# Strassen's scheme for most of the up projection, in a hybrid decoder step on one core: w_up by 7 block products in place of 8, w_up and w_down as two passes

## What is computed

```python
x = x + gt1 * mix                      # mix = merged @ w_out, 1024 x 1024
h = _rmsnorm(x, g2n) * (1 + sc2) + sh2
x = x + gt2 * (jnp.square(jax.nn.relu(h @ w_up)) @ w_down)   # w_up 1024 x 4096, w_down 4096 x 1024
y = _rmsnorm(x, g_final)
```

## Time and profile before

| | |
|---|---|
| time, median of 3 runs | 1808.45 us (1806.99 to 1808.63) |
| span of the profiled execution, first to last instruction | 1804.3 us |
| PE busy, in the span | 1775.4 us (98%) |
| VectorE, ScalarE, GpSimd busy | 759.9, 489.3, 12.3 us |
| moved by DMA | 139.34 MB, mean 77 GB/s |
| granted TensorE clock, mean | 0.995 of 2.4 GHz |

### The profile page before, as it was taken

How to read it: one execution, slowest core, us unless ns; L and a number is a source line. 1 busy time by engine, 2 the same in 40 slices (tenths; PEclk the granted TensorE clock), 3 DMA queues, 4 the chain that set the end, 5 groups by cost and what they waited for, 6 DMA issues and landing times.

```text
span 1804.3 us, 26783 instructions
## 1 busy us (share of the span) xinstructions
PE 1775.4 (98%) x10976; PEld 1713.8 (95%) x10976; DVE 759.9 (42%) x1445; ACT 489.3 (27%) x832; POOL 12.3 (1%) x25
## 2 busy tenths in 40 slices
PE   8999999999999999999999989999999999999997
PEld 3899999999999999999999989999999999999997
DVE  3644324444544545333353564343333333433345
ACT  5443333223333233211232341212121121212122
POOL 0000000000000000000000010000000000000000
PEclk9999999999999999999999989999999999999999
DMA  9444544322331232211132111111111111111112
GB/s 310 141 138 156 176 130 131 83 60 69 88 97 54 63 98 58 58 47 46 49 88 79 47 36 47 48 48 46 46 37 45 46 46 46 46 46 46 47 47 97
DMA packets 192677, 139.34 MB, mean 77 GB/s; under 512 B 15323, under 2 KB 176007, under 8 KB 192630
## 3 DMA queue, kind: packets, MB, share of 16 engines
q1 hardware_dynamic: 185910, 130.01, 24.4%
q10 hardware_dynamic: 6720, 8.67, 1.4%
HBM read 120.86 MB, written 17.80 MB: 77 GB/s over the span
## 4 chain that ended last, share of the span: by engine, by line
PE 95%; DVE 2%; DMA 1%; issue 1%; ACT 1%; SPq 0%; DVEq 0%; ACTq 0%
PE PB L916 85%; PE M L844 3%; PE M L969 1%; PE M L860 1%; PE M L1044 1%; DMA araw<-in_w_ada 1%; PE M L1050 1%; PE M L1036 1%; PE M L1038 1%; DVE XL L1223 1%; PE M L908 0%; PE M L1014 0%; DVE R L1709 0%; ACT A L532 0%; PE M L1061 0%
## 5 line engine op out<-in xcount | busy, mean ns | idle before, releaser
L916 PE MATMUL PB<-XH,whi 128*128 128x352 f32 x2496 | 811.3, 325 | 4.1 <-DVE XL L1223 2.1
L916 PE MATMUL PB<-XH,wlo 128*128 128x352 f32 x2496 | 801.5, 321 | 0.0
L916 PE MATMUL PB<-XL,whi 128*128 128x352 f32 x2496 | 801.3, 321 | 0.0
L916 PEld LDWEIGHTS PB<-XH,whi 128*128 128x128 f32 x2496 | 469.0, 188 | 11.3 <-issue 6.9
L916 PEld LDWEIGHTS PB<-XL,whi 128*128 128x128 f32 x2496 | 470.2, 188 | 0.7
L916 PEld LDWEIGHTS PB<-XH,wlo 128*128 128x128 f32 x2496 | 468.7, 188 | 0.0
L550 ACT ACTIVATE whi<-raw 128x1024 fp32r<-128x1024 f32 x134 | 141.3, 1054 | 407.4 <-PE PB L916 404.3
L916 PE MATMUL PB<-AH,whi 128*128 128x352 f32 x720 | 233.1, 324 | 0.2 <-issue 0.2
L916 PE MATMUL PB<-AL,whi 128*128 128x352 f32 x720 | 232.5, 323 | 0.0
L916 PE MATMUL PB<-AH,wlo 128*128 128x352 f32 x720 | 232.1, 322 | 0.0
L1228 DVE TENSOR_TENSOR wlo<-raw,whi 128x1024 fp32r<-128x1024 f32 x134 | 163.7, 1222 | 118.0 <-ACT whi L550 117.1
(11 more groups left out here) (297 smaller groups left out, 1199.4 us busy)
## 6 DMA issues: line engine op xcount, KB each, us to landing
raw<-in_w_in SPq DMA_DIRECT2D x64, 512.0 KB, 4.8
araw<-in_w_ada SPq DMA_DIRECT2D x48, 512.0 KB, 5.3
raw<-in_w_up SPq DMA_DIRECT2D x32, 512.0 KB, 4.0
raw<-in_w_down SPq DMA_DIRECT2D x32, 512.0 KB, 3.4
zp_d<-zr ACTq DMA_DIRECT2D x16, 512.0 KB, 2.7
Z<-zp_d SPq DMA_DIRECT2D x8, 1024.0 KB, 5.8
xin<-in_x_prompt SPq DMA_DIRECT2D x8, 512.0 KB, 7.0
CU<-in_state_C SPq DMA_DIRECT2D x8, 512.0 KB, 3.8
```

The costliest lines, as they stand in the source:

```text
L916: ins = pe.matmul(PB[:, bank, 0:BLK], w[:, w0:w0 + P], x[:, k, a0:a1], start=(k == 0 and j == 0), stop=(k == n_k - 1 and j == 2))
```

## The change

Up to the merge nothing moves. From phase 4 on:

- **Token blocks.** w_out and the first 6 tiles of w_up are computed on four blocks of 264 columns (CB) in place of three of 352: 96 matmuls of 264 columns a tile.
- **Norm.** ScalarE's root of the mean square is taken on a whole 128x264 block after one matmul with `ones` (`mean_square`), and VectorE inverts that block whole (`rstd`); GpSimd takes no part.
- **Strassen's scheme** (in Winograd's form) for the other 26 tiles, 13 pairs: a pair of output tiles by two halves of the contraction by two halves of the tokens (528 columns, two matmuls of 264) needs 7 products of 4 slices in place of 8. The sums of activations (`combo_sum`) are made once, the sums of weights (`w_sums`) per pair; the products are put together in PSUM, with three copies out (`copy_out`, ScalarE) and three sums (`product_sum`, VectorE) per pair.
- **Two passes.** All activations of w_up are written to DRAM (`act_d`, 32 tiles of 128 x 1056), as is the residual (`x2_d`); then w_down runs over all of them in the same 8 rounds of 24 groups, and reloads and splits 4 activation tiles and 4 weight tiles in each.
- The loops of these phases are written out.

```diff
+NCL = 6
+PAIRS = list(range(NCL // 2, FT * 4))
+CLG = [(c, t) for c in range(4) for t in range(4)] + [(c, t) for t in range(4, NCL) for c in range(4)]
...
+    def banks(q, which):
+        b = 4 * ((q + 1) % 2) + 2 * which
+        return PS[:, b:b + 2, 0:CB]
...
@@ SP
+        for q in range(NQ):
+            if 1 <= q < NQ - 1:
+                sp.wait_ge(s["u_lo"], 7 * q)
+                load_pair(q + 1)
+            if q >= 1:
+                sp.wait_ge(s["rl_done"], 4 * q)
+                sp.dma_start(act_d[2 * PAIRS[q - 1]:2 * PAIRS[q - 1] + 2].rearrange("a p n -> p a n"), CST[:]) \
+                  .then_inc(s["pr_out"], 16)
+        last = 7 * (NQ - 1)
+        sp.wait_ge(s["u_lo"], 7 * (NQ - 1))
+        for t in range(2):
+            load_down(t)
...
+        sp.wait_ge(s["wg_done"], last + 3)
+        for j in range(4):
+            load_act(j)
+        sp.wait_ge(s["wg_done"], last + 4)
+        sp.wait_ge(s["x2_out"], 16 * KT)
+        for n in range(4):
+            load_x2(n)
...
+        sp.wait_ge(s["pr_out"], 16 * NQ)
+        for f in range(8):
             for d in range(4):
+                t = 4 * f + d + 2
+                if t < 32:
+                    load_down(t)
+                j = 4 * f + d + 4
+                if 8 <= j < 32:
+                    load_act(j)
@@ GpSimd
-        for i, (b, k) in enumerate(POOL_H2):
...
@@ ScalarE
+        for q in range(NQ):
+            more = q < NQ - 1
+            copy_out(q, 0, T1C, 0, 3)
+            up_hi(q + 1, 0) if more else down_hi(0)
+            copy_out(q, 1, T7C, 1, 2)
+            up_hi(q + 1, 1) if more else down_hi(1)
+            copy_out(q, 2, T2C, 0, 1)
+            if more:
+                for o in range(2, 6):
+                    up_hi(q + 1, o)
+            act.wait_ge(s["wg_done"], 7 * q + 7)
+            if q:
+                act.wait_ge(s["pr_out"], 16 * q)
+            act.activation(halves(CST[:, 0, HB_:T]), banks(q, 0), ACT.Relu).then_inc(s["c12_done"], 1)
+            if more:
+                up_hi(q + 1, 6)
+        for j in range(4):
+            act_hi(j)
@@ TensorE
+        def wide_group(bank, t, c, before=None):
...
+                for j, (w, x) in enumerate(((wh, xh), (wh, xl), (wl, xh))):
+                    ins = pe.matmul(PS[:, bank, 0:CB], w[:, P * k:P * k + P], x, start=(k == 0 and j == 0), stop=(k == KT - 1 and j == 2))
+        def mean_square(c):
+            pe.wait_ge(s["sqa_done"], KT - 1 + c + 1)
...
+            pe.matmul(PS[:, SUMB[c], 0:CB], ones[:], SQA[:, CB * c:CB * c + CB], start=True, stop=True).then_inc(s["sum_done"], 1)
...
+        SEQ = ((0, True), (1, True), (0, False), (1, False), (0, False), (1, True), (0, False))
+        for q in range(NQ):
+            for o, (which, start) in enumerate(SEQ):
+                pe.wait_ge(s["u_lo"], 7 * q + o + 1)
...
+                elif 2 <= o <= 4:
+                    pe.wait_ge(s["cp_done"], 3 * q + o - 1)
+                elif o >= 5:
+                    pe.wait_ge(s["cd_done"], 3 * q + o - 4)
+                bank = banks(q, which)
+                x, wh, wl = combos(o), ring(o, 0), ring(o, 1)
                 for y in range(2):
+                    for k in range(4):
+                        for j, (w, h) in enumerate(((wh, 0), (wh, 1), (wl, 0))):
+                            ins = pe.matmul(bank[:, y, :], w[:, k, :], x[:, h, k, CB * y:CB * y + CB],
...
+        for f in range(7):
+            for n in range(KT):
+                if n % 2 == 0:
+                    pe.wait_ge(s["d_lo"], 4 * f + n // 2 + 1)
+                for b in range(3):
+                    down_group(24 * f + 3 * n + b, f, n, b,
+                               (lambda k: pe.wait_ge(s["al_lo"], 4 * f + k + 1)) if n == b == 0 else None)
@@ VectorE
+        def rstd(c):
+            x = slice(CB * c, CB * c + CB)
+            dve.wait_ge(s["rms_std"], c + 1)
+            link(dve.reciprocal(RSTD[:, x], RSTD[:, x]))
...
+        down_lo(0)
+        act_lo(0)
+        act_lo(1)
+        product_sum(q, 3, T1C, 1, 5, (0, 0))
+        act_lo(2)
+        act_lo(3)
...
+        for f in range(7):
             for d in range(4):
+                for n in (2 * d, 2 * d + 1):
+                    for b in range(3):
+                        accumulate(24 * f + 3 * n + b, n, b)
+                down_lo(4 * f + d + 2)
+                act_lo(4 * f + d + 4)
```

More of the change, by code:

```diff
@@ L82, in layer_kernel @@
     ctx = ExitStack()
-    early, startup, gates, mixer, mlstm, outp, mlp, final = (ExitStack() for _ in range(8))
+    xhs, front, early, startup, gates, mixer, mlstm, late, outp, wino, down = (ExitStack() for _ in range(11))
     def sb(name, shape, dt=F32, scope=ctx):
@@ L220, in layer_kernel @@
[L220 to L224, removed]
@@ L826, in _ @@
-        phase5(0)
-        with act.Fori(1, 7) as f:
-            phase5(f)
-        phase5(7, last=True)
+        wide_hi(T5_ + 2)
+        for k in range(KT):
+            h2_first(k)
+        square(2)
+        std(1)
+        square(3)
+        wide_hi(T5_ + 3)
+        h2_shift(1, 0)
+        h2_copy(1, 0, 1)
+        relu(0)
+        h2_shift(1, 1)
+        h2_copy(1, 1, 2)
+        std(2)
+        relu(1)
+        h2_shift(2, 0)
+        h2_copy(2, 0, 3)
+        relu(2)
+        std(3)
@@ new lines, in copy_out @@
+        def copy_out(q, o, dst, which, read):
+            act.wait_ge(s["wg_done"], 7 * q + o + 1)
+            if q == 0:
+                act.wait_ge(s["u_lo"], 7)
+            else:
+                act.wait_ge(s["cd_done"], 3 * (q - 1) + read)
+            act.activation(halves(dst), banks(q, which), ACT.Copy).then_inc(s["cp_done"], 1)
+        for o in range(7):
+            up_hi(0, o)
+            relu(17 + o)
+        act.wait_ge(s["p4_done"], 32 + len(CLG))
+        combo_hi(2, XB[:, B12, 0], B12)
@@ new lines, in down_group @@
+        def down_group(g, f, n, b, before=None):
+            a0, a1 = BLOCKS[b]
+            t = 4 * f + n // 2
+            if g >= 3:
+                pe.wait_ge(s["dn_free"], g - 2)
+            for k in range(4):
+                if before is not None:
+                    before(k)
+                w0 = 2 * P * k + P * (n % 2)
+                xh, xl = (act_tile(4 * f + k)[:, h, a0:a1] for h in range(2))
+                for j, (w, x) in enumerate(((dhi, xh), (dhi, xl), (dlo, xh))):
+                    ins = pe.matmul(PS[:, g % 3, 0:BLK], w[:, t % 4, w0:w0 + P], x, start=(k == 0 and j == 0), stop=(k == 3 and j == 2))
+            ins.then_inc(s["dn_done"], 1)
@@ new lines, in _ @@
+        for k in range(KT):
+            h2_lo_first(k)
+        residual(KT - 1, 2)
+        scaled_block(KT - 1, 2)
+        residual(KT - 1, 3)
+        scaled_block(KT - 1, 3)
+        square_sum(2)
+        wide_lo(T5_ + 2)
+        rstd(1)
+        normed(1, 0)
+        normed(1, 1)
+        square_sum(3)
+        h2_lo(1, 0)
+        relu2(0)
+        wide_lo(T5_ + 3)
+        h2_lo(1, 1)
+        rstd(2)
+        normed(2, 0)
+        relu2(1)
+        normed(2, 1)
+        h2_lo(2, 0)
@@ new lines, in _ @@
+        combo_lo(1, XT[:, 0, 1], XT[:, 0, 0], B22)
+        relu2(8)
+        combo_lo(2, XT[:, 1, 1], XT[:, 1, 0], B11)
+        relu2(9)
+        combo_lo(3, T4N[:, 1], T4N[:, 0], B21)
+        for u in range(10, 13):
+            relu2(u)
+        wide_lo(T5_ + 4)
+        relu2(13)
+        wide_lo(T5_ + 5)
+        relu2(14)
+        relu2(15)
+        w_sums(0)
+        relu2(16)
+        for o in range(7):
+            up_lo(0, o)
+            if o < 6:
+                relu2(17 + o)
+        relu2(23)
@@ L1837, in layer_kernel @@
+        for r in (6, 7, 8):
+            out(r)
     ctx.close()
```

1025 lines of the change are left out of this document (578 added, 447 removed).

## The result

The changed kernel takes 1796.59 us (median of 4 runs, 1795.89 to 1799.65) beside 1808.54 us for the kernel before on the same chip: a ratio of 0.9939, 95% interval [0.9925, 0.9953]. It is 12.0 us faster, where 21.0 were forecast; the time lies in the range (1776 to 1803).

A forecast was written before the change was run, and what follows sets the result against it. TensorE was taken as the bound. The terms summed to -21.2 us, taking the 1804.3 us span to 1783.1; with 4.2 us outside it 1787.3, stated as 1787.5, range 1780 to 1797, wider range 1776 to 1803.

The forecast's parts named there:

- rival C: At the turn to w_down, the burst of transfers runs far below 388 GB/s, giving 1795 us; chance 0.10.
- Columns and pace: On TensorE, 82,368 fewer columns at 0.4545 ns each, with 0.120 us per 264-column matmul: -37.4 us.
- Rival A: Part of each TensorE matmul doesn't shrink with the columns; decides from 0.126 us a matmul, 1823 us at 0.130; chance 0.05.
- Norm: At the second norm, 15.3 us in place of 23.1 (-7.8), and +2 us for TensorE's lower clock.
- Turn and round ends: TensorE waits on split activations: +6.7 us at the turn to w_down, +2 lower clock there, +11.3 at seven round ends.
- Rival E: Seven w_down round ends have no effect because sums out of PSUM run ahead: -11.3 us, 1776; chance 0.05.
- Rival B: TensorE's lower clock returns at every w_down round end, +14 us, giving 1801.5; chance 0.11.
- Transfers: 43 MB more DMA traffic, dense only at the turn to w_down, delaying the first tiles: +1 us (0 to 9).
- Around the span: The 4.2 us between the profiled span and the median of the runs stay, taking 1783.1 to 1787.3 us.

## Why the prediction was right, point by point

- **Direction and range** held: TensorE's columns bound the kernel, and the eighth product that Strassen's scheme saves is worth its full time. The size did not: 12.0 us for 21.0. The time, 1796.6, lies at the upper edge of the 1780 to 1797 that the forecast's own bounds gave and next to rival C's 1795, by another way than C's; that it fell into the range is in part luck.
- **Columns and pace** is the term that was mis-sized: -31.5 for -37.4. "All three are 0.455 ns a column with nothing fixed, so I take 0.120" was wrong by 1.4 ns, 4.9 us over 3528 matmuls, and my bounds of 0.119 and 0.121 did not hold it; w_down's matmuls, 0.1606 for 0.1601, add 1.2. The row at 258 columns that I leaned on the earlier trace rows is one distance: of that line's 16 distances eight are 117 or 118 ns and eight 204 or 205, a mean of 161. One short distance among uneven ones is no pace.
- **Rival A** had the right mechanism and the wrong size. The load of the stationary operand does set a floor, but at 111.7 ns, which 264 columns pass by 9.7 ns. At the 0.126 from which it would have decided, the change would have gained nothing. The rows that I chose did not show this, a load's duration of 188 ns being as misleading as a matmul's of 325; the one-column matmuls of the same trace, 0.112 us apart, would have shown it. Of the rule of the Trainium skill that I weighed ("TensorE: Matmul & The Clock Gate", section Back-to-back issue gap) the lone-matmul form gives 112.5 ns at 264 columns, an estimate, and the stream form 98.7; measured are 121.4.
- **Norm**: -3.3 for -5.8. The step that failed is the 23.1 us: 360 matmuls were taken out of the stretch where 386 stand, so 4.2 us of w_down's work were counted as norm. With 18.9 the whole forecast would have been some 1791.7. In what the new order costs I was too high: 15.6 us where 17.3 had been laid out. The reciprocal is 1.80 us, not 2.2; the waits before the four sums are 5.4 us together, where 7.7 had been laid out, and their cause was right. In the first up tiles the waits are 3.1 us for 6.6, and 2.6 of them are on ScalarE's copies, not on VectorE; the experiments too show more of the chain than VectorE: a load and ScalarE follow close behind.
- **Turn and round ends** were right in place, cause and size (+8.3 for 8.7; +13.0 for 13.1 of stops, less 1.8 for the waits of before, which here lie in its 0.1601), and the experiment that moves the splits takes all seven stops away. Rival E falls. Rival B too: the matmuls after a round's stop run at full clock (1.00 in the round shown), while the lower clock did follow the norm and the turn (0.94 in that stretch). It also fell on the first w_out tile (0.98 over the seven tiles; the first 18 matmuls, 1.6 us of the row's 1.9), but that is not the change: the run of the kernel before with 264 columns in its up tiles, untouched up to there, has it, and the changed kernel with earlier splits, the same up to there, has not. The first w_out matmuls of the two, clock third from the end:

```profile
929.31:936.00 6.69, 6.69 (x32) 6.69 (x33) 6.69 (x6) 6.69 (x8) 0.00 (x0) 0.74 0.20 60
929.72:936.00 6.28, 6.28 (x51) 6.28 (x52) 6.28 (x6) 6.28 (x8) 0.00 (x0) 1.00 0.22 65
```

- **Transfers**: no stop in the changed kernel, where 1 us was forecast. Rival C's mechanism, a low rate, was not there: the burst moves 403 GB/s from 1388 to 1400. What it would have led to, w_down's third tile late, was real nevertheless: it lay hidden under the stops at the turn, and came out as a stop of 2.4 us when the round's splits went earlier, 4.9 when the turn did and 11 with both. It was the store ahead of it in the queue that made it late.
- **Around the span** I let 4.2 us stand, which is right for a median. In the runs that give both, time less span is mostly 1.7 us; the other 2.5 are what the profiled execution of before, about 1806, lay below its median.
- **Open**: no run settles why 264 and 176 columns take some 1.5 ns more than 0.4545 a column, nor why the same start of w_out meets the lower clock in one execution and not in another.

## What to carry to other kernels

Smaller tiles cost TensorE little beyond their columns until the load of the stationary operand takes over; find that floor by cutting columns in a steady stretch, and read pace over a hundred starts, not over two. Count the matmuls of a stretch before you take their time out of it. When an activation is no longer kept but reloaded, its split becomes work with a due time: place it by the matmul that needs it, not by the loop that holds it. A wait that goes may uncover a load queued behind something unrelated; put a queue in the order of need before counting a gain.

## What the runs showed of the hardware

- A 128x128 stationary operand per matmul holds the pace at 111.7 ns, whether 176 or 224 columns move; with 64 stationary columns, 176 columns take 81.7 ns. One-column matmuls are 112 ns apart with 128 stationary columns and 85 with 96. 264 columns take 121.4 to 121.8 ns.
- A reciprocal of 264 columns on VectorE takes 1798 ns, of 16 columns 248 ns: 6.3 ns a column, less than the 8.3 ns estimated from the Trainium skill's page ("VectorE: DVE Perf Modes", section Walkthrough: the 8-slice pipeline in each mode) and than the 8 ns between one and four columns.
- The same unchanged first 930 us of the program differ by up to 3 us from execution to execution.
